# Sparse attention: the order of the head pairs on three engines, and a quarter of the query weights' low parts moved to GpSimd

## The reference

```python
q, k, v, qi, ki, wi = jnp.split(xn @ w_in, A_SPLITS, axis=-1)   # 16 query heads, 4 key/value heads, 8 index heads, of 64
q, k, qi, ki = apply_rope(...)                                   # each
score = einsum(relu(qi @ ki), wi); score = where(admissible, score, -inf)
_, sel = lax.top_k(score, 64)                                    # 64 keys for each query
logits = q . k[sel] * scale;  p = softmax(logits);  o = p . v[sel]
return from_blocks(o) @ w_o
```

## Time and profile before

| | us |
|---|---|
| median of 3 runs | 1382.57 (1382.51 to 1382.76) |
| span of the profiled execution, first to last instruction | 1381.5 |
| median less span | 1.1 |
| TensorE busy, share of the span | 1322.6, 96% |
| VectorE | 947.9, 69% |
| ScalarE | 695.3, 50% |
| GpSimd | 119.0, 9% |
| mean granted TensorE clock of the span | 0.993 |

### The profile page before, as it was taken

The page is one execution under the profiler, slowest core; times in us unless marked ns, Lnnn a source line. Parts: engine busy times, 40 slices in busy tenths (PEclk is TensorE's granted clock), DMA queues, the critical chain, the costliest instruction groups (busy, mean ns, idle before and its releaser), DMA issues.

```text
span 1381.5 us, 24879 instructions
## 1 busy us (share of the span) xinstructions
PE 1322.6 (96%) x10501; PEld 1146.3 (83%) x10501; DVE 947.9 (69%) x1419; ACT 695.3 (50%) x1185; POOL 119.0 (9%) x113
## 2 busy tenths in 40 slices
PE   4999999999999999999999997999999999999997
PEld 2997888897999888788888885788888898888886
DVE  1887798976678665675556887666556677766655
ACT  2544644444567344564444547554445567644443
POOL 0000000010101754100000130000000021000000
PEclk9999999999999999999999998999999999999999
DMA  9997799985240012355665432265655544465561
GB/s 362 375 370 240 282 360 381 353 317 165 95 151 32 4 34 94 93 177 191 185 206 173 153 126 89 83 202 180 205 184 180 160 125 151 151 200 183 183 188 56
DMA packets 177559, 256.90 MB, mean 186 GB/s; under 512 B 10472, under 2 KB 122536, under 8 KB 177448
## 3 DMA queue, kind: packets, MB, share of 16 engines
q1 hardware_dynamic: 177448, 255.31, 55.3%
HBM read 254.25 MB, written 1.05 MB: 185 GB/s over the span
## 4 chain that ended last, share of the span: by engine, by line
PE 87%; DVE 8%; ACT 2%; issue 1%; DMA 1%; SPq 0%; DVEq 0%; ACTq 0%
PE acc L2230 11%; PE acc L2232 10%; PE acc L2231 10%; PE un L2175 8%; PE un L2176 7%; PE un L2177 7%; PE side L2213 7%; PE un L2213 6%; PE side L2214 3%; PE acc L2560 3%; PE un L2214 3%; DVE w_lo L1460 2%; PE side L2560 1%; PE side L2345 1%; PE un L2560 1%
## 5 line engine op out<-in xcount | busy, mean ns | idle before, releaser
L1460 DVE TENSOR_TENSOR w_lo<-stage,w_hi 128x1024 fp32r<-128x1024 f32 (+1 forms) x374 | 450.1, 1239 | 158.0 <-ACT w_hi L869 157.1
L869 ACT ACTIVATE w_hi<-stage 128x1024 fp32r<-128x1024 f32 (+1 forms) x378 | 380.1, 1049 | 213.1 <-PE acc L2232 193.3
L2230 PE MATMUL acc<-w_hi,z_hi 128*128 128x512 f32 x640 | 253.7, 396 | 2.2 <-DVE z_lo L1907 1.3
L2232 PE MATMUL acc<-w_hi,z_lo 128*128 128x512 f32 x640 | 250.3, 391 | 0.0
L2231 PE MATMUL acc<-w_lo,z_hi 128*128 128x512 f32 x640 | 250.2, 391 | 0.0
L2175 PE MATMUL un<-h_both,w_hi 128*128 128x256 f32 x736 | 215.4, 293 | 3.5 <-DVE h_both L1518 2.2
L2176 PE MATMUL un<-h_both,w_hi 128*128 128x256 f32 x736 | 208.6, 283 | 0.0
L2177 PE MATMUL un<-h_both,w_lo 128*128 128x256 f32 x736 | 208.6, 283 | 0.0
L2175 PEld LDWEIGHTS un<-h_both,w_hi 128*128 128x128 f32 x736 | 141.5, 192 | 11.0 <-issue 6.0
L2230 PEld LDWEIGHTS acc<-w_hi,z_hi 128*128 128x128 f32 x640 | 120.7, 189 | 29.4 <-issue 3.5
L2176 PEld LDWEIGHTS un<-h_both,w_hi 128*128 128x128 f32 x736 | 141.7, 193 | 1.2 <-issue 0.7
(11 more groups left out here) (385 smaller groups left out, 1892.2 us busy)
## 6 DMA issues: line engine op xcount, KB each, us to landing
stage<-in_mlp_w SPq DMA_DIRECT2D x64, 1024.0 KB
ada_buf<-in_ada_w SPq DMA_DIRECT2D x48, 1024.0 KB, 11.2
stage<-in_w_up SPq DMA_DIRECT2D x32, 1024.0 KB
stage<-in_w_down SPq DMA_DIRECT2D x32, 1024.0 KB
stage<-in_conv_w_in SPq DMA_DIRECT2D x12, 1024.0 KB
stage<-in_rw_w_rkv SPq DMA_DIRECT2D x12, 1024.0 KB
stage<-in_w_in_a SPq DMA_DIRECT2D x8, 1024.0 KB
stage<-in_w_kv_b SPq DMA_DIRECT2D x8, 1024.0 KB
```

Source lines behind the costliest of these rows:

```text
L869: A_(w_hi[u % 2][:, half, 0:n], stage[u % NSTAGE][:, half, 0:n], ACT.Copy).then_inc(hi_made, 1)
L1460: V.tensor_tensor(w_lo[u % 2][:, half, 0:n], stage[u % NSTAGE][:, half, 0:n], w_hi[u % 2][:, half, 0:n].bitcast(F32), ALU.subtract).then_i ...
L2230: MM(y, z_hi[:, kt, q], wh[:, i, :], start=(first and kt == 0), stop=False, skip_group_check=True)
L2232: ins = MM(y, z_lo[:, kt, q], wh[:, i, :], start=False, stop=(last and kt == KT - 1), skip_group_check=True)
```

## The change

1. **Low parts.** The low parts of `U_QA+1` move from VectorE (`split(U_VA + 2)`, taken out of its queue ahead of the rope of the keys) to GpSimd, behind its cosines of the keys. GpSimd then makes three query units' low parts; ahead of those of `U_QA+3` it waits for a new semaphore, `keys_chosen`, which `sel_bias` adds to.
2. **VectorE's order.** logits(0), rope_query(1), and then in turn p: logits(p+1), four_low, shares(p), rope_query in turns 1 and 3 behind the shares, the split of `U_OA` and `U_OA+1` whole, behind the shares of turns 2 and 4.
3. **TensorE's order.** `rot_query(1)` goes between the halves of unit 7. In turn p products(p+1) comes first, then turns(p-1), filler, values(p-1). The products of pair 5 go to `un[0]`, `un[1]` too, and so wait for the rope of all four query units.
4. **Output rows.** Rows 0 and 1 of `U_OA`, both token blocks, go to turn 4; rows 2 and 3 of block 0 to turn 5 and of block 1 to turn 6. Before, block 0 stood in turn 5 and block 1 in turn 6.
5. **ScalarE's order.** `four_high` comes behind turned_out(p-1) instead of ahead of it.

```diff
-        def pair_banks(p):
-            return (acc[0], acc[1]) if p < PAIRS_BESIDE else (un[0], un[1])
+        def pair_banks(b, p):
+            return (acc[0], acc[1]) if p < (PAIRS_BESIDE if b else A_BESIDE) else (un[0], un[1])   # A_BESIDE = 5
 # GpSimd, behind the cosines of use r
-                if r in (ROPE_Q, ROPE_Q + 1):
-                    u = U_QA + 2 + r - ROPE_Q
+                if r in (ROPE_K, ROPE_Q, ROPE_Q + 1):
+                    u = U_QA + 1 + r - ROPE_K
+                    if r == ROPE_Q + 1:
+                        pool.wait_ge(sem("keys_chosen"), 1)
 # ScalarE
+                if p:
+                    pair_turned_out(0, p - 1)
                 if p in (3, 5, 7):
                     four_high(0, (p - 3) // 2)
-                if p:
-                    pair_turned_out(0, p - 1)
 # VectorE
             scores(1)
-            split(U_VA + 2)
             rope(ROPE_K, 2, kA_fm[:])
...
-            link(V.tensor_scalar(sel_bias[:], score[:], 0.5 * TAKEN, NEG, ALU.is_gt, ALU.mult))
+            V.tensor_scalar(sel_bias[:], score[:], 0.5 * TAKEN, NEG, ALU.is_gt, ALU.mult).then_inc(sem("keys_chosen"), 1)
+            dve.wait_ge(sem("keys_chosen"), 1)
+            pair_logits(0, 0)
+            rope_query(1)
             for p in range(PAIRS):
-                pair_logits(0, p)
-                if p == 0:
-                    rope_query(1)
-                if p in (2, 4):
-                    dve.wait_ge(lo_made, 2 * (U_QA + 4))
-                    split_half(U_QA + p // 2 + 3, 0)
-                    rope_query(p // 2 + 1)
+                if p + 1 < PAIRS:
+                    pair_logits(0, p + 1)
                 if p in (3, 5, 7):
                     four_low(Z_A, (p - 3) // 2)
                 pair_shares(0, p)
+                if p in (1, 3):
+                    rope_query(p // 2 + 2)
                 if p in (2, 4):
-                    split_half(U_QA + p // 2 + 3, 1)
+                    dve.wait_ge(lo_made, 2 * (U_QA + 4))
+                    split(U_QA + p // 2 + 3)
 # TensorE
             def a_products(p):
-                pe.wait_ge(rope_done, ROPE_Q + p // 2 + 1)
+                pe.wait_ge(rope_done, ROPE_Q + (N_ROPE - ROPE_Q if p >= A_BESIDE else p // 2 + 1))
...
             a_products(0)
-            a_unit(7)
+            a_half(7, 0)
+            rot_query(1)
+            a_half(7, 1)
+            a_products(1)
             z_of = z_ready(Z_A)
-            for p in range(PAIRS):
-                if p:
-                    pair_turns(0, p - 1)
-                else:
-                    a_products(1)
+            for p in range(1, PAIRS):
+                if p < PAIRS - 1:
+                    a_products(p + 1)
+                pair_turns(0, p - 1)
                 if p in (1, 2):
                     a_half(8, p - 1)
-                if p in (0, 1, 3):
-                    rot_query((p + 3) // 2)
+                if p in (1, 3):
+                    rot_query(p // 2 + 2)
+                if p == 4:
+                    pe.wait_ge(logits_read, A_BESIDE)
+                    wide_unit(U_OA, 0, z_of, rows=range(0, 2))
                 if p == 5:
-                    pe.wait_ge(logits_read, PAIRS_BESIDE)
-                    wide_unit(U_OA, 0, z_of, blocks=range(0, 1))
+                    wide_unit(U_OA, 0, z_of, blocks=range(0, 1), rows=range(2, 4))
                 if p == 6:
-                    wide_unit(U_OA, 0, blocks=range(1, 2))
+                    wide_unit(U_OA, 0, blocks=range(1, 2), rows=range(2, 4))
                 if p == 7:
                     ...
-                if 0 < p < PAIRS - 1:
-                    a_products(p + 1)
-                if p:
-                    a_values(p - 1)
+                a_values(p - 1)
```

More of the change, by code:

```diff
@@ L398, in build @@
         B_BESIDE = 7
-        PAIRS_BESIDE = 6
+        PAIRS_BESIDE, A_BESIDE = 6, 5
         U_MLP.append(add_mlp(A["w_up_2"][1], A["w_down_2"][1]))
@@ L2011, in pair_logits @@
                 for o in range(2):
-                    y, lg = flat(pair_banks(p)[o]), pair_logit[p % 2][:, o, :]
+                    y, lg = flat(pair_banks(b, p)[o]), pair_logit[p % 2][:, o, :]
                     if b:
@@ L2690, in pair_products @@
                     for o, rows in enumerate(HEAD):
-                        ins = MM(flat(pair_banks(p)[o])[:, QUERY[qt]], q_[rows, P * qt:P * qt + P], k_[rows, 0:KEYS[qt]], start=True, stop=True)
+                        ins = MM(flat(pair_banks(b, p)[o])[:, QUERY[qt]], q_[rows, P * qt:P * qt + P], k_[rows, 0:KEYS[qt]], start=True, stop=True)
                 ins.then_inc(qk_done, 1)
```

## The result

| | us | runs |
|---|---|---|
| changed kernel, median | 1387.37 (1385.09 to 1390.56) | 7 |
| kernel before, beside it | 1383.75 (1382.51 to 1384.93) | 7 |
| ratio | 1.0032 [1.0022, 1.0041] | |

The account below looks back on a forecast made before the run. The bound was taken as a ring: turns, copy, exponentials, shares, scaling, turns. turns(0) at 834.9, plus 35.7, plus clock falls of 1.3 and 0.7, put turns(6) 2.1 us later: 1382.57 + 2.1 = 1384.7 us, range 1380.3 to 1386.8.

Parts of the forecast that it names:

- The additions: VectorE's rope additions of keys, query 0, query 1: about 2.5, 2.4, 2.7 us, held by GpSimd subtractions, instead of 0.69 to 0.92.
- the single row of 0.92: VectorE addition beside GpSimd's subtraction, 0.92 instead of 0.69 us; by it alone a meeting would cost only 0.23 us.
- turns(0): Start mark of the pairs on TensorE: at 834.9, 2.3 us later than 832.64.
- turns(0) to turns(6) at full clock: TensorE's span through the pairs: 35.7 us, against 37.9 before.
- The gaps: TensorE idle ahead of products(2), ahead of products(5) (3.8 us), and in turn 5 for four_low(1) (3.1 to 3.4).
- the fall as there again ... +1.3: First fall of TensorE's clock, before turns(0)'s half unit, taken to recur at half unit 8's price: +1.3 us.
- +0.7: Clock fall behind the new 3.8 us gap: 1.7 us on the `U_OA` matmuls, 1.0 of it hidden.
- the sum: turns(6) at 834.9 + 35.7 + 1.3 + 0.7 = 872.6, 2.1 us later than 870.53.
- The bounds of 0 to 5: Clock cost on TensorE: 0 with no falls, +3.5 to +5 with both and a third behind turn 5's gap.
- third fall: Rival: another clock fall in turn 5, where TensorE waits about 3.3 us for four_low(1); +1.5 to +1.9, 1386.4 us; chance 0.17.
- What the reorder saves: Pairs, turns(0) to turns(6): 35.7 against 37.9 us, 2.2 saved, less what the clock costs.
- The base: Starting time the sum was added to: 1382.57 us, with the median 1.1 us over the profiled span.

Follow-up runs that it names:

- yield_all: Changed kernel, with GpSimd starting each of its three units' low parts only after VectorE's rope addition of the same step; ratio 1.0006 to the kernel before.
- fill_small: Changed kernel plus unread matmuls on TensorE: 4 ahead of products(2), 3 of products(5), 2 of turn 5's output rows, 1 of turns(6); ratio 1.0003 to before.
- before_fill2: Kernel before plus unread matmuls: 2 ahead of each of turns(0), turns(3), turns(4), 1 ahead of products(1), 1 in turn 5; ratio 0.9975 to before.
- lows_back: Changed kernel with the low parts of `U_QA+1` given back from GpSimd to VectorE; 1387.1 us, ratio 1.0034 to the kernel before.
- q1_first: Changed kernel, with GpSimd's second half of the third unit's low parts waiting for VectorE's query 1 addition; 1386.25 us, ratio 1.0025 to before.
- best1: yield_all plus turns(3) ahead of products(5), second block of first output rows in turn 5, four_low(1) ahead of logits(6); 1379.53 us, ratio 0.9972 to before.

## Why the prediction was wrong

- *The additions.* Forecast 2.5, 2.4 and 2.7, measured 2.61, 2.38, 2.60; `sel_bias` 0.4, measured 0.36. Right, and by the mechanism named: yield_all takes it away by moving GpSimd's start alone. The Trainium skill's rule (SBUF — State Buffer, Who interferes with whom) held each time, and the single row of 0.92 was the wrong one to size a meeting by.
- *turns(0).* Forecast 2.3 later, measured 2.31.
- *turns(0) to turns(6) at full clock.* Forecast 35.7; 35.75 in fill_small. The gaps were forecast at 3.6, 3.8 and 3.1 to 3.4 us and came at 3.7, 3.5 and 3.0.
- *The clock: the step that failed.* "the fall as there again ... +1.3" and "+0.7" make 2.0. The term was too small: taking the falls away gives 4.0 or 5.3 in time (fill_small against either ratio, each good to some 2 us), and the traces have 2.0 (37.77 - 35.75) in one execution and 5.0 in the next. The value was taken from how the kernel before had fallen once, though the new order has three gaps of 3 us and more (3.7, 3.5, 3.0) where the old one had waits for the turns of 2.6 at most. What it implied was not looked at: the same falls cost the kernel before 3.75 (37.89 - 34.12), so the sum had the new order lose 1.75 us less to the clock than the old. The runs show it losing some 0.5 to 1.8 us more, with the reserve named at before_fill2. The bounds of 0 to 5 were wide enough but for the 5.3. The "third fall" was given 0.17 and 1386.4, 3.8 above its base. It was there in one trace of two of the changed kernel, in lows_back and in q1_first, and the measured losses (4.4 and 5.7 us by the two ratios) lie nearest to it.
- *Luck in the first trace.* The profiled execution happens to be the median, 1387.37, and to have the forecast clock term of 2.0: turns(6) came 64.12 behind the end of the scores, and the sum had 64.0 (872.6 - 808.60). The next trace has 67.12, so that agreement bears nothing out. Of the 2.7 us by which this execution is over 1384.7 only 0.1 lies in the pairs: 1.6 stand at the end of the scores, 0.3 behind turns(6), and 0.7 are there because 1.8 us and not 1.1 lie outside its span. What shows the term to be too small is therefore the second trace and the ratios, not this one.
- *What the reorder saves.* "What the reorder saves is 2.2 us, less what the clock costs" set a span with 3.75 us of half level in it against one with none. With both at full clock the new order is 1.6 us longer, not 2.2 shorter: it took away 6.8 us of waiting for the turns and made 3.5 + 3.0 + 1.4 of its own behind turns(0). This changes no number of the sum, but it hid that the part meant to gain loses too, and that a gain had to come from the clock. best1, which shortens two of the new gaps, does gain.
- *The base.* The three runs shown were of the faster ones: beside the changed kernel the one before took 1383.75, and 1382.6 to 1384.0 in later sets of 15 to 27 runs. That is 1.2 of the 2.7 us between the forecast and the median. What is left, 1.5, or 2.3 by the ratio (4.4 against 2.1), fits a clock's term of 4.0 instead of 2.0, since the terms of the order came out to 0.1 us. The base trace was an early one too: its 808.60 for the end of the scores is the lowest of the fourteen traces, which go to 810.57. The profile of before had been given 1.1 us outside its span; every later execution had 1.7 to 1.9, so that profile was probably of a run near 1383.3, not of the median.

Open: why the falls differ between executions of one order. The traces show that they do (6.8 and 17.0 us at the half level), not what decides it.

## What to carry to other kernels

Before work is handed to an idle GpSimd, list the VectorE instructions with two SBUF operands that will run beside it: each may stand until a whole GpSimd instruction has ended, and a wait on GpSimd for each, which lets VectorE's go first, brings that back (here about 0.3% of the time). When a wait is moved off TensorE's queue, work out what it will wait for next at full clock in both orders, and hold the clock's price apart from that, with a range from 0 to all gaps, not one value from one trace. Where short gaps can't be closed, a few matmuls that nobody reads make the kernel faster (here 0.25% and 0.3 to 0.4%), if they are priced from a row first; the runs here also scattered less, 3.0 us in fill_small and in before_fill2 where the changed kernel's first 7 span 5.5.

## What the runs showed of the hardware

- A float32 matmul of 128x512 as a filler took 0.88 us (12.28 for 14). Products of the fast type of the same shape follow each other after 0.23 us in fill_small at full clock (starts at 855.40, 855.64, 855.86), with records of 0.39 that overlap.
- The same instructions in the same order had 6.8 and 17.0 us at TensorE's half level in two executions, and 3.0 us of difference in turns(6) from that alone. A microsecond at the half level cost 2.0 / 6.8 and 5.0 / 17.0 = 0.29 us in this ring and 3.75 / 10.2 = 0.37 in that of the kernel before, where TensorE waits anyway; near 589, in another stage, it cost (1.60 - 0.46) / 3.4 = 0.33 each.
- The hold-up between VectorE and GpSimd is not for additions only: two scalings of 128x256 in SBUF took 1.14 instead of 0.62 (yield_all), and the selection's 384 elements 1.55, 0.36 when alone.
